# Weight copies one product earlier, an early sigmoid table and later gates in a two-block kernel

## The reference

```python
u = _rmsnorm(h, mix_norm_g[l])                      # h: 16 + 512 tokens
p = u @ w_in[l]
p_pool, p_bval, p_bgate, p_cgate, p_cx = jnp.split(p, splits, axis=-1)
y_a = _pool_mixer(p_pool, pool_w[l], pool_scale[l])  # windows of 2, 4, 8, 16
y_b = _conformer_conv(p_bval, p_bgate, ...)          # v * sigmoid(g), 31 taps, layernorm, silu, @ w_pw
y_c = _rglru_branch(p_cgate, p_cx, ...)              # 4 taps, two sigmoid gates, exp, sqrt, scan, gelu
h = h + jnp.concatenate([y_a, y_b, y_c], axis=-1) @ w_out[l]
u = _rmsnorm(h, mlp_norm_g[l])
h = h + jnp.square(jax.nn.relu(u @ w_up[l])) @ w_down[l]
h = _rmsnorm(h, final_norm_g)
```

## Time and profile before

| | us |
|---|---|
| median of 3 runs | 1083.55 |
| lowest and highest run | 1081.13, 1083.64 |
| the profiled execution | 1081.01 |
| its span, first to last instruction | 1079.2 |
| PE busy | 1029.9 |
| DVE busy | 495.4 |
| ACT busy | 419.7 |
| POOL busy | 586.8 |
| mean granted clock of TensorE | 0.985 |

### The profile page before, as it was taken

The page is one execution under the profiler, slowest core; times in us unless marked ns, Lnnn a source line. Parts: engine busy times, 40 slices in busy tenths (PEclk is TensorE's granted clock), DMA queues, the critical chain, the costliest instruction groups (busy, mean ns, idle before and its releaser), DMA issues.

```text
span 1079.2 us, 12500 instructions
## 1 busy us (share of the span) xinstructions
PE 1029.9 (95%) x4959; PEld 859.2 (80%) x4959; DVE 495.4 (46%) x810; ACT 419.7 (39%) x655; POOL 586.8 (54%) x730
## 2 busy tenths in 40 slices
PE   6999999999999999999998869999999999999996
PEld 5878888888788888788898657777888888888885
DVE  2781366565446723536669784346213213312322
ACT  5343455456534324433255753353212312312232
POOL 4355555656456755457635575365645654653562
PEclk9999999999999999999999989899999999999998
DMA  6223222122432234222312112212432322332221
GB/s 219 82 88 109 79 79 77 41 78 82 162 108 78 78 124 133 95 101 79 117 40 79 39 59 78 87 51 78 133 101 78 117 84 73 117 117 78 79 78 78
DMA packets 91403, 98.61 MB, mean 91 GB/s; under 512 B 3234, under 2 KB 86720, under 8 KB 91344
## 3 DMA queue, kind: packets, MB, share of 16 engines
q1 hardware_dynamic: 91344, 97.81, 28.3%
HBM read 95.71 MB, written 2.10 MB: 91 GB/s over the span
## 4 chain that ended last, share of the span: by engine, by line
PE 77%; DVE 9%; POOL 6%; ACT 4%; issue 3%; DMA 0%; SPq 0%; DVEq 0%; POOLq 0%
PE ps L321 69%; POOL wlo L245 3%; POOL tmp L1129 2%; PE ps L662 1%; PE ps L643 1%; PE ps L787 1%; ACT whi L240 1%; POOL P L941 1%; DVE ps L1111 1%; DVE Fm L1025 1%; PE ps L600 1%; PE ps L602 1%; DVE Hl L427 1%; DVE tmp L405 1%; DMA Fm<-in_x 0%
## 5 line engine op out<-in xcount | busy, mean ns | idle before, releaser
L245 POOL TENSOR_TENSOR wlo<-raw,whi 128x256 fp32r<-128x256 f32 x672 | 501.6, 779 | 400.2 <-ACT whi L240 400.2
L321 PE MATMUL ps<-Hh,whi 128*128 128x512 f32 x848 | 334.5, 394 | 2.9 <-ACT whi L240 2.0
L321 PE MATMUL ps<-Hl,whi 128*128 128x512 f32 x848 | 331.1, 390 | 0.0
L240 ACT ACTIVATE whi<-raw 128x1024 fp32r<-128x1024 f32 x168 | 176.0, 1053 | 107.4 <-PE ps L321 91.4
L321 PE MATMUL ps<-Hh,wlo 128*128 128x512 f32 x848 | 213.2, 391 | 0.8 <-POOL wlo L245 0.8
L321 PE MATMUL ps<-Ah,whi 128*128 128x512 f32 (+1 forms) x576 | 201.1, 372 | 12.5 <-ACT whi L240 11.6
L321 PE MATMUL ps<-Al,whi 128*128 128x512 f32 (+1 forms) x576 | 197.6, 366 | 0.0
L321 PEld LDWEIGHTS ps<-Hh,whi 128*128 128x128 f32 x848 | 159.4, 188 | 37.1 <-ACT whi L240 2.4
L321 PEld LDWEIGHTS ps<-Hh,wlo 128*128 128x128 f32 x848 | 159.5, 188 | 35.1 <-POOL wlo L245 1.9
L321 PEld LDWEIGHTS ps<-Hl,whi 128*128 128x128 f32 x848 | 159.6, 188 | 32.7 <-issue 0.5
L321 PEld LDWEIGHTS ps<-Ah,whi 128*128 128x128 f32 x576 | 105.4, 192 | 33.5 <-ACT whi L240 14.4
(11 more groups left out here) (269 smaller groups left out, 905.0 us busy)
## 6 DMA issues: line engine op xcount, KB each, us to landing
raw<-in_w_in SPq DMA_DIRECT2D x36, 1024.0 KB, 5.3
raw<-in_w_up SPq DMA_DIRECT2D x16, 1024.0 KB, 5.3
raw<-in_w_down SPq DMA_DIRECT2D x16, 1024.0 KB, 5.0
raw<-in_w_att_out SPq DMA_DIRECT2D x4, 1024.0 KB, 4.9
raw<-in_w_sg_out SPq DMA_DIRECT2D x4, 1024.0 KB, 5.0
raw<-in_w_o SPq DMA_DIRECT2D x4, 1024.0 KB, 4.9
Fm<-in_x SPq DMA_DIRECT2D x2, 1024.0 KB, 6.3
Fm<-in_x SPq DMA_DIRECT2D x1, 2048.0 KB, 8.0
```

Of the source, the lines that this page charges most:

```text
L240: eh = A(lambda e, s=s, src=src, kk=kk: e.activation(wtile(whi, s, kk), src, ACT.Copy), raw_ev[b], used)
L245: el = G(lambda e, s=s, src=src, kk=kk, cut=cut: e.tensor_tensor(wtile(wlo, s, kk)[:, *cut], src[:, *cut], f(wtile(whi, s, kk))[:, *cut], ...
L321: return e.matmul(ps[:, bk, 0:c1 - c0], wt, x[:, k, c0:c1], start=st, stop=sp)
```

## The change

It computes the same. `feed(j + 3)` in place of `feed(j + 2)`: the copy of tile j+2 stands where that of j+1 stood. Banks are chosen by age, the oldest first, for single banks and pairs; the output gates, the output product and the late products then go over the four banks in the order `order4`, which starts with the pair not used last. All additions of squares are on VectorE. A new piece `table` runs a one-element sigmoid. And the pieces of `mixers` stand in other steps: the gates of group 0 one step later and one to a step, the gates of group 2 one step later (from mid C0 to the end of C0 on), more taps earlier (the last ones stand in C3, before in the first products of h = 0), `cg_lo` and the pool's pieces a step or so later, `conv_norm` and `conv_mix` each one step further apart.

```diff
-            feed(j + 2)
+            feed(j + 3)
...
+        bank_age = [0] * 8
+
+        def taken(*banks):
+            newest = max(bank_age) + 1
+            for bk in banks:
+                bank_age[bk] = newest
...
         def one_bank(n=3):
-            b = rot[0] % n
-            rot[0] += 1
-            return b
-
-        def two_banks():
-            b = 2 * (rot[0] % 2)
-            rot[0] += 1
+
+            b = min(range(n), key=lambda bk: bank_age[bk])
+            taken(b)
             return b
...
-                add = V if n == 7 else G
-                acc_ev[0] = add(lambda e: e.tensor_tensor(sq[2], sq[2], dst, ALU.add), ea, acc_ev[0])
+                acc_ev[0] = V(lambda e: e.tensor_tensor(sq[2], sq[2], dst, ALU.add), ea, acc_ev[0])
...
-            b = two_banks()
+            b = 0 if max(bank_age[0:2]) < max(bank_age[2:4]) else 2
+            taken(b, b + 1)
...
+        def table(fn):
+            A(lambda e: e.activation(sm[:, 107:108], ones[:, 0:1], fn), e_ones)
...
+            table(ACT.Sigmoid)
+            yield
             rg_gate(0, 0)
-            yield
-            rg_gate(0, 1)
             s0 = sgt_scaled(0, *made[2])
             rescale(4, 6)
             sgt_times(0, s0)
             yield
+            rg_gate(0, 1)
+            rescale(6, 7)
+            yield
             rg_gate(1, 0)
             rg_input(0)
...
             yield
+            side_taps()
+            taps(2)
+            yield
             rg_gate(2, 0)
+            scale_cg(0)
+            taps(1)
+            yield
+            rg_gate(2, 1)
...
             sp = conv_sums(*merged)
             yield
+            yield
             cn = conv_norm(sp)
             yield
+            yield
             conv_mix(cn)
...
+        order4 = (2, 3, 0, 1) if max(bank_age[0:2]) > max(bank_age[2:4]) else (0, 1, 2, 3)
...
-            evs = product([[(bk, 0, 512)] for bk in range(4)], Hh, Hl, y2, (0, 1), 2, first=False, last=(h == 0),
+            evs = product([[(bk, 0, 512)] for bk in order4], Hh, Hl, y2, (0, 1), 2, first=False, last=(h == 0),
```

More of the change, by code:

```diff
@@ L1298, in mixers @@
             yield
+            rg_gate(0, 1)
+            rescale(6, 7)
+            yield
             rg_gate(1, 0)
             rg_input(0)
+            s1 = sgt_scaled(1, *made[3])
+            rescale(7, 8)
+            sgt_times(1, s1)
             yield
             rg_gate(1, 1)
-            s1 = sgt_scaled(1, *made[3])
             rg_exps(0)
-            rescale(6, 8)
-            sgt_times(1, s1)
             yield
+            conv_input(0, *made[4])
             rg_input(1)
+            taps(2, (0,))
             rg_root(0)
             yield
-            conv_input(0, *made[4])
+            taps(2, (0,))
             rg_scan(0)
             rg_scan(1)
-            yield
-            taps(2, (0,))
+            table(ACT.Sigmoid)
             yield
@@ L1320, in mixers @@
             side_taps()
-            taps(2, (1,))
+            taps(3, (1,))
             taps(1)
@@ L1343, in mixers @@
             rg_gate(2, 1)
-            scale_cg(0)
+            side_taps()
             taps(2)
@@ L1391, in mixers @@
             side_taps()
-            taps(1)
+            taps(2)
             yield
@@ L1399, in mixers @@
             yield
-            taps(3)
+            taps(N_DVE)
             yield
-            taps(N_DVE)
             merged = conv_merge()
@@ L1419, in build @@
         cg_mm = []
-        rot[0] = 0
         for i in range(8):
@@ L1423, in build @@
             step()
+        order4 = (2, 3, 0, 1) if max(bank_age[0:2]) > max(bank_age[2:4]) else (0, 1, 2, 3)
         for c in range(4):
-            cg_mm.append(product([[(c, 16, SM)]], AMh, AMl, u2ev, mid=step)[0])
+            cg_mm.append(product([[(order4[c], 16, SM)]], AMh, AMl, u2ev, mid=step)[0])
+            taken(order4[c])
             step()
@@ L1440, in build @@
             for g in range(2):
-                product([[(2 * g, 0, 512)], [(2 * g + 1, 0, 512)]], Hh, Hl, y2, range(4, 8), 4, last=False, mid=step)
+                product([[(order4[2 * g], 0, 512)], [(order4[2 * g + 1], 0, 512)]], Hh, Hl, y2, range(4, 8), 4, last=False, mid=step)
                 step()
-            evs = product([[(bk, 0, 512)] for bk in range(4)], Hh, Hl, y2, (0, 1), 2, first=False, last=(h == 0),
+            evs = product([[(bk, 0, 512)] for bk in order4], Hh, Hl, y2, (0, 1), 2, first=False, last=(h == 0),
                           mid=step)
@@ L1451, in build @@
         for h in (1, 0):
-            evs = product([[(bk, 0, 512)] for bk in range(4)], Hh, Hl, y2, (2, 3), 2, first=(h == 0))
+            evs = product([[(bk, 0, 512)] for bk in order4], Hh, Hl, y2, (2, 3), 2, first=(h == 0))
             ea = []
-            for bk in range(5):
-                m = 4 * h + bk
-                if bk < 4:
-                    e0 = V(lambda e, bk=bk, m=m: e.tensor_tensor(F3[:, m], ps[:, bk, :], F3[:, m], ALU.add), evs[bk],
+            for i in range(5):
+                m = 4 * h + i
+                if i < 4:
+                    bk = order4[i]
+                    e0 = V(lambda e, bk=bk, m=m: e.tensor_tensor(F3[:, m], ps[:, bk, :], F3[:, m], ALU.add), evs[i],
                            x1_ev[m])
                     bank_free[bk] = e0
+                    taken(bk)
                     hm_ev[m] = e0
```

32 lines of the change are left out of this document (13 added, 19 removed).

## The result

| | before | after |
|---|---|---|
| median of the runs, us | 1082.89 (1081.13 to 1083.64, 4 runs) | 1065.73 (1063.71 to 1068.84, 4 runs) |
| ratio, 95% interval | | 0.9846 (0.9819 to 0.9874) |
| profiled execution: its time, span | 1081.0, 1079.2 | 1065.81, 1064.0 |
| first pair product P0 starts | 529.41 | 526.95 |
| first MLP product starts | 708.79 | 697.04 |

The kernel is 1.5% faster, 17.2 us by the medians; the forecast was 1067.4. The two profiled executions differ by 2 us less, 15.2: the one of before began luckily. Of the 15.2 us between the two spans 2.5 come before P0, 9.3 in the mixers and 3.4 behind them.

The account below looks back on a forecast made before the run. PE, busy 1029.9 of 1079.2 us, loses mostly idle and low-clock time in the mixers; 10.9 us there plus 5.2 elsewhere gives 16.1, so 1067.4 us; 8 in 10 range 1055 to 1078.

Parts of the forecast that it names:

- The checkpoints: Mixers walked row to row of before, each interval corrected for moved work; first MLP product at 697.9, 10.9 us earlier.
- (b): Gate (1,1) to second convolution input: 16.7 us becomes 0.3 longer, ending 577.9; new wait of about 2 us before P7.
- (c): Second convolution input to end of gate (2,0)'s sigmoid: 22.8 us plus 0.7, ending 601.4; wait of some 7 us in C1.
- (d): Gate (2,1) to gate (3,1): 8.6 us, same PE work in both kernels, so 610.1.
- (e): Gate (3,1) to pool_out(0): 34.2 us, nearly all DVE, less 4.2 for taps moved; start taken as 640.0, bounds 636 to 643.
- (f): pool_out(0) to first MLP product: 65.7 us less 7.8 (half of P9, old waits, one spell) gives 57.9.
- Before P0: Ahead of the mixers: earlier copies gain 2.1 us, oldest bank first 0.9; P0's own 0.9 us wait also goes.
- Behind the mixers: From the MLP on: half of the copies' 1.5 us, so 0.7, plus the 1.5 us wait for the sum of squares.
- More comes back: Rival, chance 0.16: DVE's chain is shorter through less POOL interference; 20 us idle and four spells go, 27 us, 1057.
- The wait moves: Rival, chance 0.16: taps brought forward cost DVE more in (b) and (c) than (e) frees; gain 5 to 10, about 1076.
- Raw weights: Rival, chance 0.07: copies wait in ACT's queue for raw blocks; four such waits with spells cost 27 us, 1095, slower.
- The early table's price: Sigmoid table load ahead of gate (2,0): row's 1.28 us saved, against the skill's extra 1380 ns drain; the row decides.

Follow-up runs that it names:

- e11: Kernel before with only the changed kernel's mixers steps and early table; copies one product ahead, banks in rotation, squares on GpSimd: 1073.10 us, ratio 0.9907.
- e4: Changed kernel with the additions of squares on GpSimd again, all but the eighth: 1069.15 us, ratio 0.9876 to the kernel before.
- e2: Changed kernel with the mixers steps of before and no early table; lead, banks and squares as changed: 1074.51 us, ratio 0.9918 to before.
- e5: Kernel before with one edit, weight copies one product further ahead (feed(j + 3)): 1081.42 us, ratio 0.9982.
- e1: Changed kernel with weight copies only one product ahead again (feed(j + 2)): 1071.39 us, ratio 0.9896 to the kernel before.
- e10: Changed kernel with pool_out one product later, taps moved late, one side_taps pair behind gate(2,0)'s sigmoid, conv_merge and conv_sums a step later: 1057.24 us, ratio 0.9762.

## Why the prediction was right, point by point

**The checkpoints.** Each interval in after's own span, with the forecast in brackets. P0 to gate(1,1): 32.2 us (560.9 less 528.5, 32.4). (b) 16.6 (17.0). (c) 22.8 before, 23.4 after, to 599.22 (23.5). (d) 8.8 (8.6). (e) 28.6 (30.0; its bounds let 26 to 33 in). (f) 60.4 (57.9). The waits named ahead were there with their sizes: 1.97 for P7 (about 2), 6.92 in C1 (some 7).

**(e)** was 1.4 us too long. The four L1139 ran at 1.31 us each as before, so that part of the bound is not it. DVE's timelines place it elsewhere: the scans of channels 2 and 3 with their multiplications took 4.81 us (617.87 to 622.68) in place of 6.44 (618.43 to 624.87), the four L1146 2.48 in place of 3.06, the mix of the first pool channel 3.36 in place of 4.18, and some 1 us was lost again at L1179, which waits 0.70 for ACT. During the scans GpSimd was busy for 3.30 of 4.81 us, before for all of 6.44; that this made them shorter is argued, not shown.

**(f) is the step that failed**, by 2.5 us. It let only P9's half, three old waits and a spell go, and didn't ask what is late next on DVE once pool_out(0) comes earlier: pool_low(1), behind the longer mix of channel 1. It made PE wait 1.97 us at 646.83, and low clock followed (0.54 and 0.63 us for the next matmuls, granted clock 0.59 from there to 651). New waits were looked for in (b) and (c) alone.

**Before P0** the copies, the bank and P0's own wait should have given 3.9 us; 2.5 were seen. The copies and banks did their part, but the first product started 0.8 us later (15.05 against 14.26) and ran at the lower clock from its fourth matmul on, seven of them at 0.63 us, about 1.4 us more. That is no effect of the change, as e11 with the short lead and the rotation has it too.

**Behind the mixers** 3.4 us came for 2.2. The waits there went as forecast, from 4.9 us to 2.7: the sum's 1.4 (e4 brings it back) and the copies' 1.5, in whose place came 0.8 for L428, so that the half taken was right. The 1.2 us beyond that I can't place. The additions moved to DVE are 18 and not twelve (page, POOL x730 to x712, DVE x810 to x828): `square_sum` also runs at the kernel's end (L1534 in before), where the wait of 1.93 us stayed as forecast.

**The sum**, 15.2 us for 16.1, came out right partly by opposite signs: (f) and the start gave less, (e), the rest before P0 and the end more. Where the forecast put the gain holds: it shortens the stretch from P0 on by 10.0 us (10.9 less P0's own 0.9), measured were 9.3, and e2 and e11 give it to the steps.

**The rivals.** *More comes back* missed: DVE's chain was as long as its rows said, but for the 1.4 us in (e), which are of the kind it named. *The wait moves* did not decide the change, but it is exactly what the lead does alone (e5). *Raw weights*: no wait of PE came from them, and behind 520 us ACT waited for no raw block, where before it did three times, up to 5.12 us. The early table's price was that of the row.

**What I would not have guessed** is e5. Read as a list of waits, says that the copies cost 13.7 us and that pool_low costs 5.3. Taking the first away moved it to the second. In these runs the copies' waits inside the stretch that a DVE chain holds were worth next to nothing (e5, and 0.7 us in e1); what the lead brings, it brings outside.

## What to carry to other kernels

Sum the waits only outside a stretch that side work holds; inside it, walk the chain of that side work from checkpoint to checkpoint, and ask at each removed wait who is late next, to the end of the stretch. Then look at the chain's own queue for work that nobody waits for (here taps ahead of the copy of a finished product, three matmuls that wait ahead of a product that is ready), and move that, but leave as much room behind as it needs.

## What the runs showed of the hardware

**VectorE and GpSimd on SBUF.** In after, L1139 (two SBUF inputs) took 1.31 us each and L1146, also with two SBUF inputs and as wide, 0.62. What differs is GpSimd, busy up to 627.87 and idle until 630.11:

```profile
623.18 5.24 DVE L1139 TENSOR_TENSOR Fm<-Fm 128x512 f32<-128x512 f32 x4
628.34 2.48 DVE L1146 TENSOR_TENSOR Hl<-Fm,Hh 128x512 fp32r<-128x512 f32 x4
```

```profile
619.40 5.06 POOL L245 TENSOR_TENSOR wlo<-raw,whi 128x256 fp32r<-128x256 f32 x4 [1.51 <-ACT whi L240]
624.42 3.45 POOL L1130 TENSOR_TENSOR tmp<-tmp 128x512 f32<-128x512 f32 x2
630.11 4.26 POOL L245 TENSOR_TENSOR wlo<-raw,whi 128x256 fp32r<-128x256 f32 x4 [2.24 <-ACT whi L240]
```

The taps, which read and write PSUM beside one SBUF input, keep 0.67 us each with GpSimd at work (four in 2.73 at 588.35, beside its L245). By the Trainium skill (SBUF — State Buffer, Who interferes with whom) a VectorE instruction with two SBUF inputs contends with a GpSimd one that reads SBUF, and the contention is an exclusive lock; these rows agree, with a factor of 2.1, and 0.62 us and GpSimd's 0.71 for a wlo part (2.84 for four at 578.36) make 1.33. Against L1139 being slow by itself speaks e11, where GpSimd ends at 634.29 and the last of the same four (L1138 there) starts at 634.8 and takes 0.675 us (durations in ns, shortest, median, longest):

```profile
L1138 DVE TENSOR_TENSOR Fm<-Fm x4: 675/1216/1777, 630.8 to 634.8; 128x512 f32<-128x512 f32 x4
```

It was read from rows, not tried by taking GpSimd's work away.

**The clock is worth nearly as much as the idle time.** Of the 9.3 us of the mixers 4.2 were idle time and some 3.5 (the estimate above) matmuls at the higher of the two levels; after a wait of 0.8 us at 350 the clock fell in one kernel and not in another. Not every spell has a wait ahead of it: when the clock fell at 675.3 us in before and at 667.8 in after (0.50 from 675.5 to 678 and from 667.8 to 671), PE had gone without a wait over 0.3 us since 663.52 and 646.83. What it had run shortly before were 32 matmuls of one column (L1211, now L1212), 3.5 us of them. At the start the first product kept the full clock in before and e10 (granted 1.00 from 15 to 20 us) and fell to the lower level in the other eleven profiles (0.70 and 0.63 in after from 15 to 17 and 17 to 20). In those two the wait ahead of it was 1.73 us and the 32 transposes ahead of the wait took 5.7 us; in the eleven it was 1.86 us or more behind transposes of 5.9 to 6.6 us, all at a granted clock of 1.00. Why the transposes took longer, and what starts a spell, is left open.
